# A transformer program's norms: square sums gathered during the projection, roots with tokens on partitions, and a new order of addresses

## The reference

```python
def rmsnorm(x, g):
    y = xf * lax.rsqrt(jnp.mean(xf * xf, axis=-1, keepdims=True) + EPS)
    return y * g

def sandwich(x, fn, pre_g, post_g, shift, scale, gate, res_w):
    hn = rmsnorm(x, pre_g) * (1 + scale[:, None, :]) + shift[:, None, :]
    y = rmsnorm(fn(hn), post_g)
    return x + res_w * gate[:, None, :] * y
```

## Time and profile before

| | |
|---|---|
| median of three runs | 3974.95 us |
| the profiled execution | 3975.63 us, span 3973.6 us, mean clock 0.961 |
| TensorE busy | 3714.3 us, 93% |
| VectorE, ScalarE, GpSimd busy | 51%, 34%, 4% |
| DMA | 426.5 MB, mean 107 GB/s |
| ScalarE's table loads (L902) | 15 of 1.28 us |

### The profile page before, as it was taken

One profiled execution on the slowest core, in us unless ns is written; L12 is line 12 of the kernel. 1 busy time (PEld: TensorE's weight loads), 2 busy tenths in 40 slices (PEclk: granted clock), 3 DMA queues, 4 the chain that ended last, 5 costly groups with the idle time before them and its releaser, 6 DMA issues.

```text
span 3973.6 us, 41625 instructions
## 1 busy us (share of the span) xinstructions
PE 3714.3 (93%) x16904; PEld 2908.8 (73%) x16904; DVE 2007.6 (51%) x3362; ACT 1362.2 (34%) x2304; POOL 159.0 (4%) x143
## 2 busy tenths in 40 slices
PE   5899999999999999979989998999899999979997
PEld 4647888657888788756668886888677777757886
DVE  7857666777666654357653335333433333344233
ACT  3553323443323322234432223222322322233222
POOL 3330000000000000001000000000000000000000
PEclk8999999989999999989999998999899999989998
DMA  6214555404555454210122222222211111112221
GB/s 247 87 53 166 202 184 185 145 28 153 202 185 199 172 191 170 80 66 27 38 69 96 96 96 69 96 96 96 67 63 58 62 63 58 54 43 85 96 96 58
DMA packets 124011, 426.53 MB, mean 107 GB/s; under 512 B 15995, under 2 KB 20987, under 8 KB 123692
## 3 DMA queue, kind: packets, MB, share of 16 engines
q1 hardware_dynamic: 123820, 423.88, 30.4%
HBM read 421.68 MB, written 2.14 MB: 107 GB/s over the span
## 4 chain that ended last, share of the span: by engine, by line
PE 86%; DVE 9%; ACT 4%; issue 1%; POOL 0%; DMA 0%; SPq 0%; DVEq 0%; ACTq 0%; POOLq 0%
PE ps L405 25%; PE ps L406 24%; PE ps L407 24%; PE ps L449 1%; PE ps L682 1%; PE ps L729 1%; PE ps L722 1%; DVE mrow L1934 1%; PE ps L772 1%; PE ps L761 1%; PE ps L528 1%; PE ps L541 0%; PE ps L521 0%; PE ps L531 0%; PE ps L662 0%
## 5 line engine op out<-in xcount | busy, mean ns | idle before, releaser
L405 PE MATMUL ps<-HH,whi 128*128 128x512 f32 x3168 | 1269.1, 401 | 80.2 <-DVE HL L1452 54.6
L406 PE MATMUL ps<-HL,whi 128*128 128x512 f32 x3168 | 1250.8, 395 | 0.0
L407 PE MATMUL ps<-HH,wlo 128*128 128x512 f32 x3168 | 1249.6, 394 | 0.0
L1416 DVE TENSOR_TENSOR wlo<-wraw,whi 128x1024 fp32r<-128x1024 f32 x526 | 644.0, 1225 | 716.2 <-ACT whi L899 715.9
L899 ACT ACTIVATE whi<-wraw 128x1024 fp32r<-128x1024 f32 x548 | 576.3, 1055 | 749.1 <-PE ps L407 742.8
L405 PEld LDWEIGHTS ps<-HH,whi 128*128 128x128 f32 x3168 | 606.3, 191 | 233.5 <-issue 92.2
L406 PEld LDWEIGHTS ps<-HL,whi 128*128 128x128 f32 x3168 | 606.6, 191 | 129.3 <-issue 4.6
L407 PEld LDWEIGHTS ps<-HH,wlo 128*128 128x128 f32 x3168 | 605.1, 191 | 129.2
L1404 DVE CUSTOM_DVE_ANT_0 mraw<-mraw,CB 128x1024 f32<-128x1024 f32 x224 | 283.1, 1265 | 1.0 <-DMA mraw<-mst 0.7
L1524 DVE TENSOR_TENSOR TT<-TT,ps 128x512 f32<-128x512 f32 x116 | 79.8, 688 | 223.3 <-PE ps L407 192.6
L407 PE MATMUL ps<-PHf,wlo 128*128 128x512 f32 x352 | 139.0, 395 | 0.0
(11 more groups left out here) (307 smaller groups left out, 3982.5 us busy)
## 6 DMA issues: line engine op xcount, KB each, us to landing
wraw<-wst SPq DMA_DIRECT2D x548, 512.0 KB, 3.4
mraw<-mst SPq DMA_DIRECT2D x224, 512.0 KB, 3.5
MR<-mst SPq DMA_DIRECT2D x16, 512.0 KB, 13.8
X<-xt SPq DMA_DIRECT2D x8, 256.0 KB, 5.9
BB<-bvec SPq DMA_DIRECT2D x8, 256.0 KB, 3.7
out<-X SPq DMA_DIRECT2D x1, 2048.0 KB, 6.3
CB<-crow SPq DMA_DIRECT2D x2, 512.0 KB, 4.8
BB<-bvec SPq DMA_DIRECT2D x8, 128.0 KB, 3.5
```

The costliest lines, as they stand in the source:

```text
L405: e.matmul(o[key], wh, sh(k), start=k == 0, stop=False)
L406: e.matmul(o[key], wh, sl(k), start=False, stop=False)
L407: ins = e.matmul(o[key], wl, sh(k), start=False, stop=k == nk - 1)
L1416: e.tensor_tensor(wlo[:, x % SPLIT, :], wraw[:, x % RAW, :], whi[:, x % SPLIT, :].bitcast(F32), ALU.subtract).then_inc(*wlo_made.up(x))
```

## The change

**Post norm.** y's gain is known before the projection, so the new X's square sum is written as the sum of x squared + 2 r (sum of g x y) + r squared (sum of g squared y squared), r being the post norm's root. During the projection ScalarE also squares the gained Y (square_gained) and VectorE adds these in SG and the cross products in SX. The eight squares of the new X and their matmuls go. In the output projections of mla and dil ScalarE copies Y from the accumulator, and squares it from there.

**Roots.** The square sums are taken with tokens on partitions: the tile of squares is stationary, a column of ones streams, and a 128x4 result holds 512 tokens. Logarithm, exponential and Newton step run on 128x4. The result is spread again by four 128x128 multiplications of the identity (diagonal) and one matmul with ones (spread), and stays in the accumulator for the modulation.

**Order.** The update of X by VectorE alone alternates with the modulation of the next stage. The FFNs' table load moves ahead of the down projection. The output is written in eight pieces.

**Addresses.** HH 16,512 to 32,896; HL to 49,280; ph from 49,280 to 129,152; X to 145,536; the raw weights to 166,016; whi to 178,304; wlo to 190,592; the rest behind.

```diff
-        X = sb("X", [P, 8, S])
         HH = sb("HH", [P, 8, S], F32R)
         HL = sb("HL", [P, 8, S], F32R)
+        ph = (pos[0] + 127) // 128 * 128
+        pos[0] = ph + 79872
+        X = sb("X", [P, 8, S])
         wraw = sb("wraw", [P, RAW, BT * 128])
...
-        ph = (pos[0] + 127) // 128 * 128
...
+            def sums(o, src, rhs, at_, first=False):
+                for j in range(4):
+                    ins = e.matmul(o[:, 4 * j + at_:4 * j + at_ + rhs.shape[1]], src[:, 128 * j:128 * j + 128], rhs,
+                                   start=first and j == 0, stop=j == 3, skip_group_check=True)
+                return ins
+
+            def spread(s, banks):
+                o = take(("root", s), banks)
+                lane.wait_ge(v_norm, ("dg", s))
+                e.matmul(o, C["ones"][:], T[0] if s[0] == "q" else T[2], start=True, stop=True).then_inc(*mm_done.up(("root", s)))
...
             def post_norm(layer, sub, last=False):
-                norm_total(("q", layer, sub))
...
+                ins = sums(o, SQ[:], one, 0, True)
                 if not last:
-                    square_total(("p", layer, sub + 1) if sub < 2 else ("p", layer + 1, 0))
+                    lane.wait_ge(v_norm, ("sga", s, 6))
+                    sums(o, SG, one, 1)
+                    lane.wait_ge(v_norm, ("sxa", s, 6))
+                    x = take(("totx", s), cross_bank)
+                    ins = sums(x, SX, one, 0, True)
+                ins.then_inc(*mm_done.up(("tot0", s)))
+                lane.wait_ge(a_norm, ("sq", s, 7))
+                sums(o, T[1], one if last else GV[:], 0).then_inc(*mm_done.up(("toty", s)))
+                if not last:
+                    lane.wait_ge(v_norm, ("sxy", s, 7))
+                    sums(x, T[4], one, 0).then_inc(*mm_done.up(("totx", s)))
+                spread(s, root_bank)
+                if not last:
+                    spread(("p", layer, sub + 1) if sub < 2 else ("p", layer + 1, 0), next_bank)
...
+            def diagonal(s, k, dst):
+                for j in range(4):
+                    ins = e.tensor_scalar(dst[:, 128 * j:128 * j + 128], C["ident"][:], tok[k + 3][:, j:j + 1], None, ALU.mult)
...
             def modulate(s, v, idx, after=None, update=None):
...
                     e.scalar_tensor_tensor(T[m % 5], X[:, m, :], AM[:, idx, m:m + 1], R, ALU.mult, ALU.mult).then_inc(
                         *v_norm.up(("b", s, m)))
+                    if m < 6 and update is not None:
+                        update(m + 2)
                     if m:
                         low(m - 1)
...
+            def cross(s, m, y):
...
+                e.scalar_tensor_tensor(T[4] if m else SX, y, GM[:, idx, m:m + 1], X[:, m, :], ALU.mult, ALU.mult).then_inc(
+                    *v_norm.up(("sxy", s, m)))
+                if 1 <= m < 7:
+                    lane.wait_ge(v_norm, ("sxy", s, m))
+                    e.tensor_tensor(SX, SX, T[4], ALU.add).then_inc(*v_norm.up(("sxa", s, m)))
...
+                    e.tensor_tensor(u, tot[:, 1, :], r, ALU.mult).then_inc(*v_norm.up(("u0", s)))
...
+                    e.scalar_tensor_tensor(u, total_of(("totx", s))[:, 0, :], 2.0, u, ALU.mult, ALU.add).then_inc(*v_norm.up(("u1", s)))
...
+                    e.tensor_tensor(u, u, r, ALU.mult).then_inc(*v_norm.up(("u2", s)))
...
+                    e.tensor_tensor(u, u, ms, ALU.add).then_inc(*v_norm.up(("u3", s)))
...
+                    e.tensor_scalar(ms, u, 0.0, None, ALU.max).then_inc(*v_norm.up(("ms", z)))
...
             for m in range(8):
-                lane.wait_ge(x_by[m], ("x", ("q", 1, 2), m))
-            e.dma_start(out, X[:]).then_inc(*x_out.up("x"))
+                lane.wait_ge(v_norm, ("x", ("q", 1, 2), m))
+                e.dma_start(out[:, m, :], X[:, m, :]).then_inc(*x_out.up("x"))
```

More of the change, by code:

```diff
@@ L995, in ffn @@
                         product(tag, i, conv)
+                    if half == 1:
+                        table("natural_log_exp_and_others")
                     for m in range(8):
@@ L1425, in square_add @@
                         lane.wait_ge(v_norm, ("sqa", s, m - 1))
[L1426 to L1438, removed]
+                    e.tensor_tensor(SQ[:], SQ[:], T[m % (2 if s[0] == "q" else 4)], ALU.add).then_inc(*v_norm.up(("sqa", s, m)))
@@ L1446, in amul, with modulate @@
                     *v_norm.up(("am", idx)))
-            def modulate(s, v, idx, R):
+            def modulate(s, v, idx, after=None, update=None):
+                R = bank(("root", s))
                 def low(m):
@@ L1474, in pre_norm @@
                 amul(idx, v + 1, gain_of("pre", 3 * layer + sub))
[L1475 to L1480, removed]
-                lane.wait_ge(v_mod, ("mod", v))
[L1482 to L1486, removed]
+                single(s)
@@ L1501, in post_norm @@
-                add(prev)
+                lane.wait_ge(mm_done, ("root", s))
+                if stage in ("mla", "dil"):
+                    lane.wait_ge(a_norm, ("y", s, 7))
+                freed[("root", s)] = ((v_norm, ("yn", s, 7)),)
+                if last:
+                    for m in range(8):
+                        update(m)
+                else:
+                    update(0)
+                    update(1)
+                    modulate(z, v, nxt, s, update)
             def residual(key, v, m, name):
@@ L1547, in ffn @@
                         product(tag, i, conv)
+                    if half and gate is None:
+                        gains(s)
                     for m in range(8):
@@ L1550, in ffn @@
                         feed(11)
+                        if half:
+                            square_add(s, m - 1)
                         if gate is not None:
@@ L1982, in vector_engine @@
             mod_step(0)
-            rsqrt(s, R)
+            lane.wait_ge(c_in["ident"], "in")
+            single(s)
             lane.wait_ge(v_mod, "amb")
+            lane.wait_ge(mm_done, ("root", s))
+            R = bank(("root", s))
+            freed[("root", s)] = ((v_norm, ("b", s, 7)),)
             def low(m):
@@ L2186, in sync_engine @@
             e.dma_start(WAX[:], wax).then_inc(*wax_in.up("wax"))
-            const_in([n for n, w in CONST_WIDTHS if n != "ones"])
+            const_in([n for n, w in CONST_WIDTHS if n not in ("ident", "ones")])
             feed(160)
```

223 lines of the change are left out of this document (139 added, 84 removed).

## The result

After: 3937.22 us, median of 4 runs (3935.53 to 3941.97); before, in the same session, 3975.30 (4 runs). The ratio is 0.9906, 95% interval 0.9889 to 0.9923. The forecast of 3992 was wrong in sign, and its range (3935 to 4010) holds the result only at its lower end, where two rivals had stretched it.

What follows compares the result with a forecast made beforehand. TensorE, holding 86% of the chain that ended last, was taken to bound the kernel. 3975.6 - 35 (Term 1) + 0.5 (Term 2) - 3.5 (Term 3) + 55 (Term 4) = 3992.6, stated as 3992 us; range 3935 to 4010.

Steps and rivals of the forecast that it cites:

- two rivals: Two alternatives inside the range: addresses do nothing, 3938 (chance 0.06); a high stationary operand costs half, 3955 (0.08).
- Term 4: Addresses: split weights move high, so every projection matmul runs at the high pitch and the products gain nothing: +55 us.
- an operand that lies high costs: Projection matmuls: an operand at a high address, moving or stationary, costs about 6.6 ns each (0.2267 to 0.2333).
- Those nine steps: Row-wise projection with CH and CW stationary and high: nine matmul steps at 0.2333, read as a high stationary operand's cost.
- The first rival: Projections: only the moving operand's place counts, so HH and HL keep 0.2267 and products fall to it: 3915; chance 0.14.
- The second rival: Projections: the place does nothing, the pitch has another cause, and only the norms count: 3938; chance 0.06.
- Term 1: Five double norms (post norm followed by pre norm): TensorE restarts sooner, 7 us won at each, 35 in all.
- the wait for wlo: Behind each double norm: after 48 matmuls TensorE waits some 3 us for the next split of weights.
- Term 2: Single norms (four behind residual projections, and the first): 0, between -1 and +1 each; +0.5 at the start.
- Term 3: Program's end, from the last projection matmul on: output in pieces, the last of 256 KB, and a shorter norm: -3.5 us.

Runs made afterwards that it cites:

- e1: Kernel before, with the products' region begun 128 bytes further on (148,352 instead of 148,224): 3953.36 us, ratio 0.9948.
- e4: Changed kernel, with the products' region 128 bytes further on (49,408, still low) and all that follows 256 bytes further: 3955.76 us, ratio 0.9957.
- e5: Kernel before, with the two buffers of split weights 128 bytes further on (86,272 and 98,560), other alignments kept: 3998.98 us, ratio 1.006.
- e8: Kernel of e3 with all its buffers 128 bytes further on, their distances kept: 3906.07 us, ratio 0.9829.
- e2: Changed kernel with its norms but the address order of before (X first, products' region last, at 148,480): 3960.42 us, ratio 0.9965.
- e3: Changed kernel, with the split of one block of weights moved from behind the modulation to the wait for the totals: 3907.84 us, ratio 0.9834.
- e6: Kernel before, with the products' buffers moved by pair of FFNs: both by 64 bytes, both by 32, or PL alone by 128: 3969.22 us, one run.
- e7: Changed kernel, with ScalarE's silu table load moved from each FFN's start to behind the splits of its first weights: 3926.17 us, ratio 0.9876.
- e11: Kernel of e10 with the table load moved as in e7: 3886.37 us, ratio 0.9775.
- e10: Kernel of e3 plus matmuls that serve nothing behind the last spread (12 at double norms, 5 at single ones): 3890.74 us, ratio 0.9793.

## Why the prediction was wrong

**Term 4 was the error of sign**: +55 forecast, -21 measured. The two pitches were read rightly (0.2333 against 0.2267). The step that failed is "an operand that lies high costs": one difference between HH and the products was taken for the cause. The addresses stood beside it and had another: 32,896, 49,280, 86,144 and 98,432 all leave 128 when divided by 256, and 148,224 leaves 0. That reading also explains, with stationary CH at 164,608 (remainder 0) against moving weights (128), and with it the change brings the products' region to 49,280 and the weights to 166,016, remainder 128 both: all fast. e1, e4, e5 and e8 show it for the projections that move HH and the products. Those nine steps of the earlier trace rows were few, as the prediction said: in e1, where CH and the weights agree, the same nine take 2.08 us, 0.231, since they stand just behind a wait and haven't settled to 0.2267. The size was off as well. In e5 HH does run at the slow pitch, and its cost in time is 23 + 21 = 44 where 55 was forecast.

The first rival had the products' 21 right, but by a false mechanism: e4's products move from a low place and are slow. The Trainium skill's sentence behind it (TensorE: Matmul & The Clock Gate, "Step-by-step: what each phase is for"), two read ports that are independent of each other, doesn't foresee that the pair of addresses matters; here the measurement decides: HH moves at 0.2267 or 0.2333 with nothing changed but the weights' start (e5). The second rival, "the place does nothing", gave 3938, within 1 of the result, by coincidence: it had the pitch unchanged and the norms at 38.

**Term 1 was mis-sized**: -35 forecast. The profiled execution shows -48.8 + 29.2 + 11.0 = -8.6; by the medians of e2 and e4, less the end's 4, it is -9 and -14. The gaps came as forecast (17.7 on average for 17.2), and the wait for wlo was named. The forecast's own mark was the start of the third block, 33.0 behind the last projection matmul instead of 40.2. It came at 34.2 on average instead of 40.2: 30 us were still there. The missing 5 are the table load ahead of ScalarE's split at a1, b0 and b1 (1.28 each; it stands in the earlier trace rows at the other end of the stage) and the gaps, 0.5 longer each. Then 10 are lost behind the third block's start, in the second low stretch (some 12 x 0.2 = 2.4 at each of three places, 1.4 at the fourth, and slower restarts; e4's execution has only one of them), and 11 in the rest of the latent and dilated stages, whose cause is open. More matmuls ran low behind the restart too, 11 to 13 instead of the 9 that were taken, but the wait for the split takes that up. The step that failed: the prediction counted a wait as the time until its releaser and took the full clock behind it for granted. With the early split the same norms are worth 3953.4 - 3907.8 = 45.5 (e1 to e3), of which 4 are the end: 41, a little above the 35.

**Term 2** (0, within 1 each): the gaps are 9.75, 9.99, 9.93 and 9.26 for 9.06, 9.15, 9.11 and 9.15, +2.5 in all. **Term 3** (-3.5): -4.1. Both held.

## What to carry to other kernels

Before an address is blamed, write down the starts of both operands of a fast and a slow matmul and compare their remainders, not only their size; one kernel with the suspect moved by 128 bytes costs a line and would have turned this forecast. When a wait on the way to TensorE is shortened, follow the work that the waiting engines have behind it (splits, table loads) up to where the next buffer runs out, and look at the granted clock behind each wait: 49 us won in the gaps were worth 9 to 14 until one block's split was moved into them. Matmuls that serve nothing pay where they leave only a short idle stretch ahead of the restart; more of them, earlier, gained at the single norms and lost at the double ones.

## What the runs showed of the hardware

- A 128x128 by 128x512 fp32r matmul comes each 0.2267 us if the two operands' starts in the partition agree modulo 256, and each 0.2333 if they differ by 128 or 192, 0.2343 by 160 (moving start less stationary start; e1, e4, e5, e6, e8). Where they lie makes no difference (49,280 or 148,352). A distance of 256 modulo 512 is fast too (86,144 to 148,352 in e1). Why isn't shown, and other distances weren't tried.
- Behind the restarts of the five double norms of one execution the number of matmuls at the low clock varies from 5 to 13 (e3). The length of a second wait doesn't tell whether a low stretch follows: 12 matmuls behind 3.6 us (the changed kernel), 7 behind 3.5 (e7), none behind 3.9 and 3.8 (e4), none behind 2.7 and 7 behind 2.3 (the changed kernel).
- Kernels with the new norms scatter more, 6 to 24 us between a kernel's runs, with the second waits (e2: 22, e4: 6) and without them (e3: 13, e11: 24); e1's five lie within 2, before's within 1 to 9. Why isn't shown.
- Matmuls of 128x512 ahead of the restart, twelve at the double norms and five at the single ones, in a wait that was there anyway, saved 17 us over nine boundaries (e3 to e10).
